# Activation tables of ScalarE set by hand in a two-block transformer kernel

## The reference: what is computed

```python
x = x + gt1 * hybrid_mixer(modulate(rmsnorm(x, g_norm1), sh1, sc1), ...)   # conv branch (silu), 4-head mLSTM, gates (sigmoid)
x = x + gt2 * hierarchical_moe(modulate(rmsnorm(x, g_norm2), sh2, sc2))    # 32 experts, silu(gate) * up, top 2 of one group
x = rmsnorm(x, g_final)
h = h + deltanet_mixer(rmsnorm_2(h, a_norm))      # silu(conv), l2norm of q and k, softplus and exp gates, chunks, rmsnorm of o
h = h + conv_ffn(rmsnorm_2(h, f_norm[0]))         # (silu(gate) * up) @ w_down, 2816 wide
h = h + swa_sink_attention(rmsnorm_2(h, b_norm))  # softmax over a band of 128
h = h + conv_ffn(rmsnorm_2(h, f_norm[1]))
out = rmsnorm_2(h, final_norm)
```

## Time and profile before

| | |
|---|---|
| median of 3 runs | 2426.91 us (2420.43 to 2429.96) |
| the profiled execution, its own time | 2416.55 us |
| its span, first to last instruction | 2414.8 us |
| TensorE (PE) busy with matmuls | 2205.4 us, 91% |
| VectorE (DVE) busy | 1199.1 us, 50% |
| ScalarE (ACT) busy | 821.2 us, 34% |

### The profile page before, as it was taken

One profiled execution on the slowest core, in us unless ns is written; L12 is line 12 of the kernel. 1 busy time (PEld: TensorE's weight loads), 2 busy tenths in 40 slices (PEclk: granted clock), 3 DMA queues, 4 the chain that ended last, 5 costly groups with the idle time before them and its releaser, 6 DMA issues.

```text
span 2414.8 us, 29742 instructions
## 1 busy us (share of the span) xinstructions
PE 2205.4 (91%) x11694; PEld 1573.3 (65%) x11694; DVE 1199.1 (50%) x1768; ACT 821.2 (34%) x1287; POOL 118.0 (5%) x160
## 2 busy tenths in 40 slices
PE   7999998679999999798994989999999899999997
PEld 3788656433333333366784877888887687888885
DVE  4799575400000000158657345777725563877822
ACT  4222452311212112244653344333424374323422
POOL 0000000021111111100003000000000000000000
PEclk9999999889999999989997689999999899999999
DMA  9442205539999999711110012222223201222221
GB/s 380 168 174 96 76 3 210 208 154 410 397 415 407 395 421 406 299 70 70 70 70 1 2 43 97 105 91 83 105 105 137 73 1 70 105 104 89 85 105 70
DMA packets 35351, 384.54 MB, mean 159 GB/s; under 512 B 9024, under 2 KB 9280, under 8 KB 12352
## 3 DMA queue, kind: packets, MB, share of 16 engines
q1 hardware_dynamic: 27520, 374.89, 39.2%
q0 software_dynamic: 7744, 8.44, 1.0%
HBM read 381.85 MB, written 14.73 MB: 164 GB/s over the span
## 4 chain that ended last, share of the span: by engine, by line
PE 58%; DMA 9%; DVE 5%; ACT 4%; issue 3%; POOL 0%; POOLq 0%; ACTq 0%; SPq 0%; DVEq 0%
PE PS L628 14%; PE PS L630 14%; PE PS L629 14%; DMA A<-h_tokens,idx 7%; PE PS L868 5%; PE PS L830 2%; PE PS L875 1%; PE PS L998 1%; DMA h<-wexp 1%; PE PS L820 1%; ACT A L1424 1%; PE PS L1191 1%; PE PS L588 1%; PE PS L823 0%; PE PS L913 0%
## 5 line engine op out<-in xcount | busy, mean ns | idle before, releaser
L628 PE MATMUL PS<-h_hi_r,w_hi_r 128*128 128x512 f32 x1056 | 423.5, 401 | 11.6 <-DVE A L1822 5.0
L629 PE MATMUL PS<-h_r,w_hi_r 128*128 128x512 f32 x1104 | 432.7, 392 | 0.0
L630 PE MATMUL PS<-h_hi_r,ring_r 128*128 128x512 f32 x1056 | 413.4, 391 | 0.0
L2103 DVE TENSOR_TENSOR ring_r<-ring,w_hi_r 128x1024 fp32r<-128x1024 f32 x196 | 238.6, 1222 | 339.9 <-ACT w_hi_r L1434 339.8
L1434 ACT ACTIVATE w_hi_r<-ring 128x1024 fp32r<-128x1024 f32 x196 | 206.0, 1057 | 457.3 <-PE PS L630 284.0
L628 PEld LDWEIGHTS PS<-h_hi_r,w_hi_r 128*128 128x128 f32 x1056 | 199.7, 189 | 65.9 <-issue 12.7
L629 PEld LDWEIGHTS PS<-h_r,w_hi_r 128*128 128x128 f32 x1104 | 209.7, 190 | 47.1 <-issue 4.7
L630 PEld LDWEIGHTS PS<-h_hi_r,ring_r 128*128 128x128 f32 x1056 | 199.5, 189 | 42.6
L2092 DVE TENSOR_TENSOR A<-A,PS 128x512 f32<-128x512 f32 x16 | 11.0, 687 | 390.0 <-PE PS L830 390.0
L830 PE MATMUL PS<-A 128*64 128x512 f32 x768 | 170.1, 599 | 0.1
L1822 DVE SCALAR_TENSOR_TENSOR A<-A,vec 128x511 f32<-128x511 f32 (+15 forms) x216 | 160.1, 741 | 6.7
(11 more groups left out here) (468 smaller groups left out, 3516.1 us busy)
## 6 DMA issues: line engine op xcount, KB each, us to landing
A<-wexp SPq DMA_DIRECT2D x64, 2048.0 KB, 12.5
ring<-wall SPq DMA_DIRECT2D x63, 2048.0 KB, 8.1
ring<-wexp SPq DMA_DIRECT2D x16, 2048.0 KB, 19.0
h<-wexp SPq DMA_DIRECT2D x16, 2048.0 KB, 19.1
A<-wada SPq DMA_DIRECT2D x12, 2048.0 KB, 14.6
x<-xt_in SPq DMA_DIRECT2D x2, 2048.0 KB, 10.3
A<-y_assignments SPq DMA_DIRECT2D x4, 1024.0 KB, 7.9
h_tokens<-A SPq DMA_DIRECT2D x4, 512.0 KB, 2.8
```

What stands on the lines that cost most here:

```text
L628: mm(out, w[0], x_[0], start=first, stop=False)
L629: mm(out, w[0], x_[1], start=False, stop=False)
L630: return mm(out, w[1], x_[0], start=False, stop=last_)
L2103: tt(ring_r[:, slot, :, cols], ring[:, slot, :, cols], w_hi_r[:, :, cols].bitcast(F32), ALU.subtract).then_inc(S("w_lo"), 1)
```

## The change

`LN_EXP` is loaded ahead of each stretch of Ln and Exp, `SILU` ahead of the loops and behind the stretches inside the delta-rule projections. Loads are still put in automatically where a function is not in the table then loaded. `SIGMOID` is never used. One thing besides loads moves: the eight Exp of m = 18 now stand at m = 17, behind the eight Ln.

```diff
+            LN_EXP, SIGMOID, SILU = 6, 2, 18
+            def table(number):
+                nc.scalar.add_instruction(mybir.InstLoadActFuncSet(name=nc.get_next_instruction_name(), engine=mybir.EngineType.Activation, act_func_set_id=number))
...
             a_(silc[:], V("c", 0, KD), ACT.Silu).then_inc(S("eps"), 1)
+            table(LN_EXP)
             norm(0)
...
+            table(LN_EXP)
             act.wait_ge(S("cl_mm"), 2)
...
                         a_(A[:, 40 + i, :], A[:, 40 + i, :], ACT.Silu, bias=V("conv_ln_b", i)).then_inc(S("ya_in"), 1)
+                    table(LN_EXP)
...
             a_(rs[8], rs[8], ACT.Exp).then_inc(S("rexp"), 1)
+            table(SILU)
             n = doubles(act)
...
+            table(LN_EXP)
             for j in range(4):
                 w_hi(NU1, j)
...
                 if m == 4:
+                    table(LN_EXP)
                     act.wait_ge(S("ab_ev"), 3)
...
                     a_(glast[:], R("a_gate")[:, DH:2 * DH], ACT.Exp).then_inc(S("ab_a"), 1)
+                    table(SILU)
...
                 if m == 17:
+                    table(LN_EXP)
                     for i in range(8):
                         act.wait_ge(S("l_ev"), i + 1)
                         a_(l_sum[i], l_sum[i], ACT.Ln, bias=eps[:, 0:1]).then_inc(S("l_ln"), 1)
-                if m == 18:
                     for i in range(8):
                         act.wait_ge(S("l_ln"), i + 1)
                         a_(l_sum[i], l_sum[i], ACT.Exp, scale=-0.5).then_inc(S("l_r"), 1)
+                    table(SILU)
...
                     if g == 6 and j == 0:
+                        table(LN_EXP)
...
+                        table(SILU)
+            table(LN_EXP)
...
+                table(SILU)
                 with act.Fori(0, FU // 2) as i:
...
                 unit(FU - 1, 0, FU // 2)
+                table(LN_EXP)
                 act.wait_ge(S("mm"), UNIT_USED[f"up{layer}_{FU - 1}"])
```

## The result

The changed kernel takes 2400.49 us in the median of 4 runs (2400.00 to 2406.45), the kernel before beside it 2424.83 us (4 runs, 2420.43 to 2429.96): a ratio of 0.9905, 95% interval 0.9878 to 0.9931. Two further sets gave 0.9929 (0.9908 to 0.9951) and 0.9926 (0.9907 to 0.9944). So the change makes the kernel faster by 0.7 to 1.0%, 17 to 23 us by these ratios.

What follows compares the result with a forecast made beforehand. TensorE, busy 91% of the span, was taken as the bound, so loads count only where it waits. Gains of 13.7 us less a cost of 2.9 gave -10.8 us, 2426.9 to 2416.1 us; range 2406 to 2424 us.

Steps and rivals of the forecast that it cites:

- drain rival (-27 us): Each load also holds ScalarE for a drain of 1.38 us: some -27 us, 2400 us; chance 0.02.
- rival that hand-made loads come on top of the automatic ones: Seams gain nothing and the mLSTM, m = 4 and m = 17 cost more: +9.4 us, 2436.3 us; chance 0.06.
- `norm(0)`, -0.8: First norm: without loads the copy behind the Exp waits only for TensorE's own sums, so the chain gains 0.8 us.
- rival of the clock: Shorter waits at seven places may spare half-rate stretches, m = 17 cost less: -14 to -16 us, about 2411.5 us; chance 0.15.
- mLSTM -1.3, head norms and `norm(1)` -2.6: One load fewer at the mLSTM's start, 1.3 us; earlier last tile at head norms, 1.2; bare Exp load at norm(1), 1.4.
- Experts 0: Experts' loop: its loads went into idle time before 16 Silu, so removing them gains 0.
- ninth pass: Other rounding moves a token to another expert and the experts' loop runs once more: +54.5 us, 2481.4 us; chance 0.02.
- `norm(3)` to m = 6, -3.7: VectorE gets norm(3)'s Exp earlier and m = 4 has two loads instead of three; TensorE's wait ends 3.7 us earlier.
- m = 17, +2.9: Eight Ln and eight Exp in one block delay the Square; TensorE stands 3.7 us, half clock behind it: cost 2.9 us.
- Second Ln and Exp, 0: Second eight Ln and Exp: three loads become two, but the weight piece behind them comes at the same moment: 0.
- Delta rule, -4.0: Eight loads go; only the last two `o_factor` count, and TensorE's waits of 5.99 and 3.86 us end 4.0 us earlier.
- Feed-forward loops, 0: Both feed-forward loops with their 20 loads: TensorE is never idle there, so whatever ScalarE saves gains 0.

Runs made afterwards that it cites:

- e13: Changed kernel plus one more joint-table load between Ln and Exp at norm(0): 2407.94 us, the changed kernel beside it 2403.10 us.
- e14: Kernel before plus one joint-table load ahead of norm(0) alone: 2416.60 us against 2421.31 us, ratio 0.9981.
- e4: Kernel before with the joint table ahead of norm(0), ahead of the mLSTM and in its first head only: 2414.32 against 2425.42 us, ratio 0.9955.
- e3_m17: Kernel before with only the change's block at m = 17 (joint table, eight Ln, eight Exp, Silu table): 2423.47 against 2425.42 us, ratio 0.9995.
- e2: Kernel before with the Silu table set ahead of the experts' and each feed-forward loop, nothing else: 2422.04 against 2425.42 us, ratio 0.9994.
- e8: Changed kernel with 120 loads added, 88 in the feed-forward parts and 32 in the experts: 2403.81 us, the changed kernel beside it 2403.34 us.
- e1_delta: Kernel before with one joint-table load behind the gate tiles, removing the delta rule's eight loads: 2416.64 against 2425.42 us, ratio 0.9967.
- e7_m4: Changed kernel, eight Exp back at m = 18 behind weight piece and Square, m = 4's weight piece ahead of its block: 2399.29 us, 0.9915 to kernel before.
- e11_price: Changed kernel with one more load between Ln and Exp at norm(0) and two more at norm(7): 2417.78 us in one run.

## Why the prediction was wrong

By its own steps:

- *Number, kind and price of the loads*: right. 22 stand against 77, each 1283 ns, the joint table too. The drain rival (-27 us) and the rival that hand-made loads come on top of the automatic ones are out.
- *`norm(0)`, -0.8*: **this term failed.** The wait shrank as worked out, by 0.73 us, but the stretch by 3.0 us: the other 2.3 us are the same matmuls at a higher clock, which the term put at nothing. The words that failed are in the rival of the clock: I priced "TensorE's clock gives more than it takes" as one or two spared half-rate stretches somewhere, gave it 0.15, and argued against it that "most of the waits stay over 2.7 us". The wait that mattered was a short one, 1.45 to 0.72 us, and from the matmul behind it to the input projection all ten profiles with the joint table at `norm(0)` and nothing added there have 64.0 to 64.2 us where the five without have 65.6 to 66.9. Both directions were timed (e13, e14).
- *mLSTM -1.3, head norms and `norm(1)` -2.6*: right, 1.5 and 2.3 us. e4's 11 us is these and `norm(0)`, by the stretches 6.8 us; the remainder up to the interval's lower edge of 8 us is not explained.
- *Experts 0*: right that nothing is swallowed, and no ninth pass came (528.6 us in the first changed profile, 528.2 before). The stretch scatters by 4.5 us in the six profiles as before and by 7.2 us in the ten as changed; its -1.1 us is within that. A change of 3 us in one profile, which the forecast named as a sign of being wrong, could not have told anything.
- *`norm(3)` to m = 6, -3.7*: right, 3.8 us.
- *m = 17, +2.9*: right in mechanism and size, 2.5 us; the 3.7 us wait was 3.5 us. 1.1 us of it are waits and 1.4 us busy time, as the half clock was priced.
- *Second Ln and Exp, 0*: right. They lie in the row m = 17, which is as long in e3_m17 with the first block alone (102.4 us) as in the changed kernel (102.4 to 102.6).
- *Delta rule, -4.0*: right mechanism, size too small. The waits gave what was worked out (6.0 to 2.5 us; the short one of 0.5 us at the chunk before went as well), but the stretch gained 5.3 us: the eight matmuls behind the shorter wait took 1.09 instead of 1.97 us in nine of eleven profiles. It is the step of `norm(0)` again.
- *Feed-forward loops, 0*: right, with 120 loads to spare (e2, e8). The -0.8 us of that row is not the loops' and not the work right behind the delta rule: its first 40 us are 0.2 us longer as changed, and 0.9 us go in the attention, 1907 to 2011 us. e1_delta, the delta rule's loads alone, has 975.7 us and e2_loops 976.5; but e7_m4 with the whole change has 976.7. What it hangs on is open.
- *`norm(7)`, -1.3*: right, 1.4 us.

So about 3.5 of the 6.3 us between forecast (-10.8) and stretches (-17.1) are one omission, the clock at two places (2.3 and 1.2 us); the rest is the experts' scatter (1.1), the 0.8 us above and small differences. Of the further 9.3 us from 2416.1 to 2400.5 us a part is the starting point: I took the difference off 2426.9 us, the median of three runs. In four sets of 11 to 30 runs the kernel before has medians of 2421.3 to 2425.4 us and a spread of 16 to 17 us. Another part is chance on the other side: the changed kernel's first median of four, 2400.5 us, was 2.6 us and more under its later ones. The changed kernel's 16 runs spread by 9 us, from 2400.0 to 2409.2 us.

What stays open: why the medians of the first set differ by 24 and those of the others by 18 to 19 us; what the rest of e4's 11 us is; why one wait of 1.36 us (e13) is followed by more time at half rate than one of 1.45 us (before), and so whether it is the length of the wait that counts or the moment at which it falls; and which of the two lengths the start of the chunks takes.

## What to carry to other kernels

A table load counts only where TensorE stands still for it: of the 55 loads removed, 28 in the loops gained nothing measurable, and 154 us of added ones cost nothing, while one at the first norm cost some 5 us. Where one function block must stand ahead of work that another engine waits for, look at the order before the count: spreading the block at m = 17 and moving a weight piece ahead of the one at m = 4 took the time from 2403 to 2395 us with the same 22 loads. And price a wait of TensorE with the clock behind it; here a short one, 1.36 or 1.45 us between groups of small matmuls, cost more by the clock than by itself.

## What the runs showed of the hardware

- Behind a wait of 1.36 or 1.45 us at `norm(0)`, 16 matmuls that take 1.92 us at the 2.4 GHz level took up to 3.64 us, and the next 64 us of work became 65.6 to 69.8 us; behind one of 0.72 us the work took 64.0 to 64.2 us in every profile. The granted clock over that work was 0.85 to 0.92 against 0.94 to 0.95.
- A switch of table costs 1.28 us and no more than 0.03 us around it (e11_price), also for the table that holds both Ln and Exp; a load of the table that is already there costs the same 1.28 us (e13_one_load).
- Executions of one program differ by up to 17 us: by the start (first matmul at 10.7 to 12.9 us), by the experts' stage (526 to 534 us, in which TensorE is busy for 482 to 494 us with the same matmuls), and by two lengths at the start of the chunks (42.4, or 44.7 to 45.8 us).
